# FFN-in units of a macaron decoder layer: T3's sum made by an adding DMA, T2's and T4's by VectorE at the ends

## The reference

```python
x = x + 0.5 * swiglu_ffn(rmsnorm(x, ffn1_norm), ffn1_w_in, ffn1_w_out)
...
x = x + mixed @ w_out            # mixer: dilated attention and forgetting attention
x = x + 0.5 * swiglu_ffn(rmsnorm(x, ffn2_norm), ffn2_w_in, ffn2_w_out)

def swiglu_ffn(x, w_in, w_out):
    gate, up = jnp.split(x @ w_in, 2, axis=-1)
    return (jax.nn.silu(gate) * up) @ w_out
```

## Time and profile before

| | |
|---|---|
| runs | 1764.17, 1765.71, 1765.87 us; median 1765.71 |
| profiled execution | 1765.33 us, its span 1763.4 us |
| TensorE, VectorE, ScalarE busy | 99%, 84%, 63% of the span |
| granted TensorE clock | 1.00 (2.4 GHz) in every unit of the span |
| a unit of full width | 41.55 us: TensorE busy 41.40, VectorE 37.5, ScalarE 28.4; DMA share 0.88 at 266 GB/s |

### The profile page before, as it was taken

One profiled execution on the slowest core, in us unless ns is written; L12 is line 12 of the kernel. 1 busy time (PEld: TensorE's weight loads), 2 busy tenths in 40 slices (PEclk: granted clock), 3 DMA queues, 4 the chain that ended last, 5 costly groups with the idle time before them and its releaser, 6 DMA issues.

```text
span 1763.4 us, 21396 instructions
## 1 busy us (share of the span) xinstructions
PE 1749.3 (99%) x7976; PEld 1449.7 (82%) x7976; DVE 1475.3 (84%) x1769; ACT 1109.2 (63%) x1461; POOL 100.2 (6%) x117
## 2 busy tenths in 40 slices
PE   9999999999999999999999999999999999999999
PEld 7788888888888888888888888888888888888887
DVE  7899989998899998575755655898899999899998
ACT  7676666666666666554445545666676676666665
POOL 0100010000000001100000000100000000000000
PEclk9999999999999999999999999999999999999999
DMA  9998888886754556555455546888888987865762
GB/s 377 307 285 273 267 254 262 262 254 193 270 215 177 218 214 208 171 200 171 163 185 164 176 168 255 276 262 263 261 273 267 278 277 213 260 213 168 257 216 88
DMA packets 169190, 408.30 MB, mean 232 GB/s; under 512 B 9112, under 2 KB 18352, under 8 KB 163584
## 3 DMA queue, kind: packets, MB, share of 16 engines
q1 hardware_dynamic: 154208, 342.03, 53.7%
q0 software_dynamic: 13760, 62.94, 17.7%
q10 hardware_dynamic: 1120, 1.97, 0.3%
HBM read 351.57 MB, written 5.79 MB: 203 GB/s over the span
## 4 chain that ended last, share of the span: by engine, by line
PE 87%; DVE 5%; DMA 3%; issue 2%; ACT 2%; SPq 1%; POOL 0%; ACTq 0%; DVEq 0%
PE bank L666 7%; PE bank L694 7%; PE bank L696 7%; PE bank L695 7%; PE bank L627 7%; PE bank L629 7%; PE bank L628 6%; PE bank L668 6%; PE bank L667 6%; PE bank L774 5%; PE bank L776 5%; PE bank L775 5%; PE bank L800 3%; PE bank L801 3%; PE bank L802 3%; DVE wlo L1323 2%
## 5 line engine op out<-in xcount | busy, mean ns | idle before, releaser
L1323 DVE TENSOR_TENSOR wlo<-raw,whi 128x1024 fp32r<-128x1024 f32 (+1 forms) x506 | 608.1, 1210 | 196.0 <-ACT whi L970 186.1
L970 ACT ACTIVATE whi<-raw 128x1024 fp32r<-128x1024 f32 (+1 forms) x506 | 527.8, 1048 | 348.6 <-PE bank L629 183.8
L694 PE MATMUL bank<-whi,xs 128*128 128x512 f32 (+1 forms) x608 | 237.5, 391 | 0.7 <-DVE wlo L1323 0.4
L695 PE MATMUL bank<-wlo,xs 128*128 128x512 f32 (+1 forms) x608 | 234.4, 386 | 0.0
L696 PE MATMUL bank<-whi,xs 128*128 128x512 f32 (+1 forms) x608 | 234.4, 385 | 0.0
L970 ACT ACTIVATE whi<-tsum 128x1024 fp32r<-128x1024 f32 (+1 forms) x120 | 122.0, 1035 | 96.5 <-PE bank L696 65.1
L774 PE MATMUL bank<-whi,aw_hi 128*128 128x512 f32 x420 | 164.0, 391 | 0.0
L776 PE MATMUL bank<-whi,aw_lo 128*128 128x512 f32 x420 | 163.5, 389 | 0.0
L775 PE MATMUL bank<-wlo,aw_hi 128*128 128x512 f32 x420 | 163.4, 389 | 0.0
L1323 DVE TENSOR_TENSOR wlo<-tsum,whi 128x1024 fp32r<-128x1024 f32 (+1 forms) x120 | 141.8, 1195 | 24.8 <-ACT whi L970 23.1
L627 PE MATMUL bank<-whi,xs 128*128 128x512 f32 x384 | 155.1, 404 | 0.4 <-DVE wlo L1323 0.4
(11 more groups left out here) (221 smaller groups left out, 3129.4 us busy)
## 6 DMA issues: line engine op xcount, KB each, us to landing
raw<-ffn_w_in SPq DMA_DIRECT2D x86, 1024.0 KB, 6.9
raw<-ffn_w_out SPq DMA_DIRECT2D x84, 1024.0 KB, 6.8
raw<-w_in SPq DMA_DIRECT2D x48, 1024.0 KB, 5.0
raw<-ffn_w_in SPq DMA_DIRECT2D x75, 512.0 KB, 7.0
tsum<-raw POOLq DMA_DIRECT2D x36, 1024.0 KB, 6.9
minis<-ffn_w_in SPq DMA_DIRECT2D x72, 256.0 KB, 7.1
last_plain<-ffn_w_in SPq DMA_DIRECT2D x36, 512.0 KB, 6.1
raw<-w_out SPq DMA_DIRECT2D x16, 1024.0 KB, 4.9
```

What stands on the lines that cost most here:

```text
L694: mm(banks[b][:, 0:w], xs[:, k + i, 0, tok], hi, start=starts[b] and k + i == 0, stop=False, skip_group_check=True)
L695: mm(banks[b][:, 0:w], xs[:, k + i, 0, tok], lo, start=False, stop=False, skip_group_check=True)
L970: A(whi[:, h % SLOTS, 0:n_el], src, ACT.Copy).then_inc(weights_hi, 1)
L1323: V.tensor_tensor(wlo[:, h % SLOTS, 0:n_el], src, whi[:, h % SLOTS, 0:n_el].bitcast(f32), ALU.subtract).then_inc(weights_lo, 1)
```

## The change

T3's sum is taken from VectorE and made by two adding DMAs (B22 onto B12, within SBUF), issued by GpSimd between those of T2 and T4, with the wait `t3_added` on ScalarE. In the first unit of the first FFN VectorE makes T2's sum, in the last unit of both FFNs T4's. `swiglu` moves behind both low parts of B11, and the turning moves behind GA's product.

```diff
+            def add_b22(u, j):
+                n12, n22, w = unit_piece(u, j, "B12"), unit_piece(u, j, "B22"), UNIT_W[j]
+                pool.wait_ge(sums_done, 2 * ((UNITS - 1) * u + j))
+                pool.wait_ge(raw_full[raw_slot(n22)], RAW_FULL[n22])
+                pool.dma_start(raw[:, raw_slot(n12), 0:4 * w], raw[:, raw_slot(n22), 0:4 * w], accum_op=ALU.add).then_inc(t3_added, 16)
+                pool.dma_start(minis[:, raw_slot(n12), 0:w], minis[:, raw_slot(n22), 0:w], accum_op=ALU.add).then_inc(t3_added, 16)
...
             for j in range(1, UNITS):
-                add_piece(0, j, "B22", T1_B11, t2_added)
-                add_piece(0, j, "B21", T2_B21, t4_added)
+                if j > 1:
+                    add_piece(0, j, "B22", T1_B11, t2_added)
+                add_b22(0, j)
+                if j < UNITS - 1:
+                    add_piece(0, j, "B21", T2_B21, t4_added)
...
             for j in range(1, UNITS):
                 add_piece(1, j, "B22", T1_B11, t2_added)
-                add_piece(1, j, "B21", T2_B21, t4_added)
+                add_b22(1, j)
+                if j < UNITS - 1:
+                    add_piece(1, j, "B21", T2_B21, t4_added)
...  TensorE
                 form(base + B11, Y, a11, w, False, True)
-                act_turn(u, j - 1)
                 pe.wait_ge(copied, 3 * first + 1)
                 plain(base + GA, 0, (Z, X), (False, True), w, -1)
+                act_turn(u, j - 1)
                 plain(base + GB, 2, (Z, X), (False, True), w, -1)
...  ScalarE
-                act_e.wait_ge(t2_added, 32 * (first + 1))
+                if first == 0:
+                    act_e.wait_ge(t_summed, 3)
+                else:
+                    act_e.wait_ge(t2_added, 32 * first)
...
-                    act_e.wait_ge(sums_done, 4 * first + 3 + i)
+                    act_e.wait_ge(t3_added, 32 * (first + 1))
                     split(base + T3 + i, form_half(n12, i, w), w2)
...
-                act_e.wait_ge(t4_added, 32 * (first + 1))
+                if j == UNITS - 1:
+                    act_e.wait_ge(t_summed, 3 * (u + 2))
+                else:
+                    act_e.wait_ge(t4_added, 32 * ((UNITS - 2) * u + j))
...  VectorE: sum_t3 goes; new:
+            def sum_t2(u, j, i):
+                n22, w = unit_piece(u, j, "B22"), UNIT_W[j]
+                if i == 0:
+                    full(n22)
+                    dve.wait_ge(weights_lo, unit_half(u, j) + T1_B11 + 1)
+                V.tensor_tensor(t_half(i, w), form_half(n22, i, w), t_half(i, w), ALU.add).then_inc(t_summed, 1)
+                if i:
+                    V.tensor_tensor(tmini[:, 0:w], form_last(n22, w), tmini[:, 0:w], ALU.add).then_inc(t_summed, 1)
+
+            def sum_t4(u, j, i):
+                n21, w = unit_piece(u, j, "B21"), UNIT_W[j]
+                if i == 0:
+                    dve.wait_ge(weights_lo, unit_half(u, j) + T2_B21 + 1)
+                V.tensor_tensor(t_half(i, w), form_half(n21, i, w), t_half(i, w), ALU.add).then_inc(t_summed, 1)
+                if i:
+                    V.tensor_tensor(tmini[:, 0:w], form_last(n21, w), tmini[:, 0:w], ALU.add).then_inc(t_summed, 1)
...
-                split(base + B11, form_half(n11, 0, w), w2)
+                for i in range(2):
+                    split(base + B11 + i, form_half(n11, i, w), w2)
                 swiglu(u, j - 1)
-                split(base + B11 + 1, form_half(n11, 1, w), w2)
                 plain_split("GA", GA)
-                sum_t3(u, j, 0)
+                if first == 0:
+                    sum_t2(u, j, 0)
                 plain_split("GB", GB)
-                sum_t3(u, j, 1)
+                if first == 0:
+                    sum_t2(u, j, 1)
...
                 split_two(base + T2_B21, tmini[:, 0:w], form_last(n21, w), w)
+                if j == UNITS - 1:
+                    sum_t4(u, j, 0)
                 plain_split("GC", GC)
+                if j == UNITS - 1:
+                    sum_t4(u, j, 1)
```

More of the change, by code:

```diff
@@ L374, in layer @@
         x_stored, x_back = sem("x_stored"), sem("x_back")
-        sums_done, t2_added, t4_added, copied, w_done, gate_added, c11_done = (
-            sem(n) for n in ("sums_done", "t2_added", "t4_added", "copied", "w_done", "gate_added", "c11_done"))
+        sums_done, t2_added, t3_added, t4_added, t_summed, copied, w_done, gate_added, c11_done = (
+            sem(n) for n in ("sums_done", "t2_added", "t3_added", "t4_added", "t_summed", "copied", "w_done", "gate_added", "c11_done"))
         sq_done, hss_ready, hms_ready, hr_ready, hsc_ready, qn_ready, qk_psum, qkT_ready, v_ready = (
@@ L1121, in unit @@
                 for i in range(2):
-                    act_e.wait_ge(sums_done, 4 * first + 1 + i)
+                    act_e.wait_ge(sums_done, 2 * first + 1 + i)
                     split(base + T1 + i, t_half(i, w), w2)
@@ L1499, in sum_t1 @@
                 done.then_inc(sums_done, 1)
-            def sum_t3(u, j, i):
-                n12, n22, w = unit_piece(u, j, "B12"), unit_piece(u, j, "B22"), UNIT_W[j]
+            def sum_t2(u, j, i):
+                n22, w = unit_piece(u, j, "B22"), UNIT_W[j]
                 if i == 0:
                     full(n22)
-                    dve.wait_ge(sums_done, 4 * ((UNITS - 1) * u + j - 1) + 2)
-                done = V.tensor_tensor(form_half(n12, i, w), form_half(n22, i, w), form_half(n12, i, w), ALU.add)
+                    dve.wait_ge(weights_lo, unit_half(u, j) + T1_B11 + 1)
+                V.tensor_tensor(t_half(i, w), form_half(n22, i, w), t_half(i, w), ALU.add).then_inc(t_summed, 1)
                 if i:
-                    done = V.tensor_tensor(form_last(n12, w), form_last(n22, w), form_last(n12, w), ALU.add)
-                done.then_inc(sums_done, 1)
+                    V.tensor_tensor(tmini[:, 0:w], form_last(n22, w), tmini[:, 0:w], ALU.add).then_inc(t_summed, 1)
[6 more added lines that the diff above has]
+                    V.tensor_tensor(tmini[:, 0:w], form_last(n21, w), tmini[:, 0:w], ALU.add).then_inc(t_summed, 1)
             def plain_unit(u):
```

## The result

The changed kernel takes 1800.09 us (median of 4 runs, 1797.74 to 1802.69) against 1765.13 before: ratio 1.0196, 95% interval 1.0183 to 1.0208. It is 35 us slower, where 4.5 us less were forecast, and lies above the range given. The profiled execution took 1800.77 us, its span is 1799.0.

What follows compares the result with a forecast made beforehand. TensorE, busy 99% of the span, was taken as the bound, with 8.1 us of waits for low parts of weights. 1.93 + 2.96 - 0.4 = 4.5 us won gave 1760.8, or 1761.2 as median; range 1758.5 to 1784.

Steps and rivals of the forecast that it cites:

- the part on T3's adding DMA: Full units: T3's add hidden, UA just in time, T4's add landing near 206.2 against 206.7 wanted; cost nothing, bound 66 us.
- the count for UA: Load packets of B12 and UA, 896 in all, counted beside the adds: UA lands at 203.8 to 204.9, needed by 204.87.
- The chain from UA to UC without slack: VectorE from UA's split to UC's low part: each microsecond UA lands after 204.87 is lost, in 17 units.
- rival one: UA comes late: with half the packets beside the adds it lands at 207.3, 42 us lost, 1803 us; chance 0.24.
- The prediction's own sign of being wrong: ScalarE waiting at UA or T4 in every unit, units over 41.9 us, or ScalarE waiting for T3's DMA beyond 199.4.
- The second rival: Adds and loads take turns in blocks, nothing overlaps: T4's add lands at 208.6, 32 us lost, 1793 us; chance 0.05.
- rows 11 and 12: First unit's queue counts before the change: 35 load packets beside 47 of an add in 2 us, 139 beside 131 in 2.5.
- The ends: VectorE's T2 sum in the first unit wins 1.93 us, T4's in the last units 2.96, less 0.4 lost: 4.5 us.
- The move: `swiglu` behind B11's low parts: wait moves to GA, 0.31 us, costing nothing in 18 units; bounds 7.6 us won, 1.8 lost.
- VectorE's sums: T3's sums taken from VectorE, 1.2 + 1.2 + 0.6 us in each full unit, off the path: nothing won.

Runs made afterwards that it cites:

- The kernel with the backlog and only two adds: Changed kernel with T3's sum back on VectorE, and SyncE holding the next unit's B12, then UA and UB, until T2's first low part is made: 1811.94 us.

## Why the prediction was wrong

**The step that failed** is in the part on T3's adding DMA: "T4's add is issued at 196.61 and starts some 1.1 us later as T2's does", and from it "T4's add lands near 206.2". It started when the loads issued before it had run out, 3.4 us after its issue in the unit shown (2.6 to 4.1 in the 17 units), its last packets were held up again by the next loads, and it landed 2.7 us after ScalarE wanted it. The kernel with the backlog and only two adds shows that this delay needs no third add; the kernel with B12 late shows that the third add costs nothing without it. What the third add does is to hold up the loads of B12, UA and UB until T4's add is due. I had counted these loads to see when UA would land, let 378 of them run between T3's and T4's add, left 123 to 155 for the time beside T4's, and never asked what they do to the start of T4's. With UB's 256, which the count for UA had no need of, some 380 to 410 would still have been queued at that start by my own figures; in the trace it is some 480, since B12's first packet came 4.5 us after its issue (228.88, 233.43) and not 3.1. The 1.1 us taken for an add's start were short as well: 1.4 without loads.

**The price was right, the victim was not.** The chain from UA to UC without slack, a loss of one for one in 17 units, is what happened, with 1.07 to 3.29 us in the units compared. I had priced it for UA (rival one, chance 0.24, 1803 us). UA came in time, so that rival's mechanism is wrong, and that its time is near is luck. The prediction's own sign of being wrong, "ScalarE waits for a load at UA or for `tmini` at T4 in every unit, units of over 41.9 us", came true in its second half. The second rival (blocks, 0.05, 1793 us) named T4's lateness, put at 1.9 us; it was right that the add and the loads don't overlap there, wrong that they never do, as beside T3's add they did.

**The packet counts.** Beside T3's add the two queues went nearly one to one, 98 and 93 packets in 4 us, as rows 11 and 12 had it. The Trainium skill ("DMA: Bandwidth & Descriptors", "Queues, rings and completion order") has a DMA engine go round the queues that it has work for and drain a whole packet, typically 9 to 17 descriptors, before it switches. The 98 and 93 agree with going round for two queues that are both running; over 16 engines they are some 6 of each in 4 us, which leaves no room for blocks of that size if a packet of the profile is one descriptor. The rule by itself gives no delay of 2 to 3 us for an add that comes late, and the 541 against 1 don't agree with it, unless the add's work had not reached the engines by then. No row shows when it does beside loads; without them its first packet comes after 1.4 us.

**The ends were right.** 4.5 us forecast, 5.5 measured alone. The 0.2 us that I took off in each last unit show in no wait, and are too small to see in the times.

**The move was right in its place and near in its size.** The wait went from B11 to GA as computed, with a gap of 0.40 us in place of 0.31. I took the move at nothing, with 1.8 us lost as the bound. The medians put it at 2.5 us lost (1762.61 against 1760.10, T3 on VectorE in both), but their intervals, 0.9970 to 0.9988 and 0.9960 to 0.9983, overlap; the gaps in the traces differ by 0.09 us in each full unit, 1.4 us together. That the turning's 0.79 us ahead of GA would cover it was right, and worth more than the 8 us expected: 10.3.

**VectorE's sums** won nothing where they went, as forecast: 1751.55 and 1752.35 us with and without T3's DMA.

**Does the sum close?** By the medians T3's DMA alone loses 43, the ends win 5.5, the move loses 2.5: 40 us, but the whole change lost 35. With the profiled execution of the kernel with T3's DMA alone, which lost 38, it is 35. Why that kernel's other three times are 3 to 7 us higher stays open.

## What to carry to other kernels

When a DMA is added, ask what it pushes into the time of the next one: here it was not the new transfer that TensorE was held up by but the one after it, behind loads that the new one had held up. A share of DMA time near 1.0 says little; what decides is whether loads are queued at the moment at which an urgent transfer is issued, and the order in which loads are issued can keep that moment free. A late low part can be hidden by work of TensorE that needs no weights, put right before it, as the turning did here.

## What was not expected of the hardware

Two queues that were both running moved nearly equal counts of packets (98 and 93 in 4 us), but an add that was issued behind loads began only as these ran out. T4's add moved nothing while 435 packets of loads ran (2.1 us), and one packet beside 541 in 3 us. Its first packet came 1.4 us after the issue behind some 120 packets of loads, 2.1 us behind 450 and 3.4 us behind 700. The other way round it is not the same: B12's loads, issued at 228.88 behind the adds of T2 and T3, began 4.5 us later, when all 128 large packets of T3's add were still to come. So a queue that comes late does not always wait for all that the other has. What in the engines makes it so stays open, and no run here changed the size of the packets or put more than some 870 of them ahead of an add.

Issuing 1280 KB of loads behind the add, and UC's ahead of B22's, took away all of the 37 us. Three adds and all loads of a unit ran at a DMA share of 1.03 and 298 GB/s in 41.6 us, and TensorE stood still 0.25 us.
